# Five token blocks (256, 256, 256, 128, 128 + 32) in place of four (256, 256, 256, 256 + 32) in the front half of a hybrid decoder step

## The reference

```python
h = rms_norm(x, norm1_g)
proj = h @ w_in + b_in
att = windowed_attention(q, k, v, sinks)          # window 128, 8 query heads, 2 kv heads
rw, wkv_t, shift_t = rwkv7_time_mix(proj[...])    # a recurrence over the tokens
merged = gate_a * (att @ w_up_a) + gate_b * (rw @ w_up_b)
x = x + merged @ w_o
h2 = rms_norm(x, norm2_g)
x = x + peer_ffn(h2)      # per token: 8 heads, each picks 16 of 16384 experts by two lists of 128 keys
y = rms_norm(x, final_norm_g)
```

## Time and profile before

| | |
|---|---|
| median of 3 runs | 4102.34 us |
| the profiled execution's own time | 4110.9 us |
| span of its trace | 4109.1 us |
| busy: PE, DVE, POOL, ACT | 79%, 69%, 36%, 35% |
| mean DMA rate over the span | 326 GB/s |
| chain that ended last: PE, DMA, DVE, issue | 23%, 18%, 8%, 6% |

### The profile page before, as it was taken

How to read it: one execution, slowest core, us unless ns; L and a number is a source line. 1 busy time by engine, 2 the same in 40 slices (tenths; PEclk the granted TensorE clock), 3 DMA queues, 4 the chain that set the end, 5 groups by cost and what they waited for, 6 DMA issues and landing times.

```text
span 4109.1 us, 40924 instructions
## 1 busy us (share of the span) xinstructions
PE 3259.7 (79%) x12315; PEld 2054.4 (50%) x12315; DVE 2854.3 (69%) x5892; ACT 1417.6 (35%) x3794; POOL 1478.0 (36%) x1330
## 2 busy tenths in 40 slices
PE   7699779878897788688986975898998867657666
PEld 6487456356655553465654633675554422222221
DVE  1442257878866788798864785795866976688676
ACT  1421123623433346234532353232433332233232
POOL 0210123465323334663331443463322344444443
PEclk9799889989999898899998987997899998998988
DMA  4004699978999899699997995786898999999998
GB/s 152 19 1 134 246 346 372 357 271 318 352 385 406 330 382 360 262 376 376 421 381 303 356 351 204 291 355 257 328 363 322 420 421 421 421 419 417 410 417 331
DMA packets 249647, 1341.30 MB, mean 326 GB/s; under 512 B 32537, under 2 KB 67225, under 8 KB 113474
## 3 DMA queue, kind: packets, MB, share of 16 engines
q0 software_dynamic: 152064, 1107.36, 67.4%
q1 hardware_dynamic: 97362, 231.32, 15.3%
HBM read 1306.90 MB, written 32.70 MB: 326 GB/s over the span
## 4 chain that ended last, share of the span: by engine, by line
PE 23%; DMA 18%; DVE 8%; issue 6%; ACT 2%; POOL 2%; SPq 1%; DVEq 0%; POOLq 0%; ACTq 0%
DMA ring<-in_uv_dram,expert_id 15%; PE acc L2261 8%; PE front L1022 4%; DVE ring L2159 3%; PE front L1077 2%; PE front L766 2%; DVE y_dve L2058 2%; PE front L1040 2%; DMA weights_in<-in_w_all_dram 1%; POOL ring L2033 1%; DMA big<-bonus_gate 0%; ACT diag L2228 0%; PE front L747 0%; DVE ch_xy L1678 0%; DVE ch_alv L1638 0%
## 5 line engine op out<-in xcount | busy, mean ns | idle before, releaser
L2033 POOL DMA_INDIRECT ring<-in_uv_dram,expert_id x1056 | 1224.2, 1159 | 2361.8 <-PE acc L2261 1324.6
L2261 PE MATMUL acc<-ring,diag 128*128 128x512 f32 (+1 forms) x2704 | 1449.3, 678 | 466.8 <-ACT diag L2228 434.7
L2159 DVE CUSTOM_DVE_ANT_0 ring<-ring,h_tile 128x1024 f32<-128x1024 f32 x1056 | 1287.3, 1240 | 264.7 <-DMA ring<-in_uv_dram,expert_id 207.1
L2261 PEld LDWEIGHTS acc<-ring,diag 128*128 128x128 f32 (+1 forms) x2704 | 537.5, 211 | 1183.9 <-ACT diag L2228 577.6
L2058 DVE SCALAR_TENSOR_TENSOR y_dve<-ring,weights,y_dve 128x1024 f32<-128x1024 f32 x371 | 482.7, 1301 | 116.5 <-ACT weights L2216 103.9
L2212 ACT ACTIVATE acts<-dots 128x2 f32<-128x2 f32 x528 | 107.4, 203 | 818.5 <-DVE dots L2159 744.9
L766 PE MATMUL front<-hT,weights_in 128*128 128x257 f32 (+7 forms) x1280 | 304.6, 395 | 18.9 <-DVE hT L1483 18.9
L766 PEld LDWEIGHTS front<-hT,weights_in 128*128 128x128 f32 (+2 forms) x1280 | 243.1, 191 | 88.3 <-DVE hT L1483 21.8
L1077 PE MATMUL front<-h2T,weights_in 128*128 128x256 f32 (+1 forms) x1024 | 250.7, 401 | 31.2 <-DMA weights_in<-in_w_all_dram 30.5
L2216 ACT ACTIVATE weights<-acts,gate 128x1 f32<-128x1 f32 x1056 | 254.1, 288 | 17.4 <-ACT acts L2212 0.2
L2228 ACT ACTIVATE diag<-ident,weights 128x128 f32<-128x128 f32 x651 | 240.2, 390 | 20.5 <-POOLq L521 12.7
(11 more groups left out here) (346 smaller groups left out, 4051.1 us busy)
## 6 DMA issues: line engine op xcount, KB each, us to landing
weights_in<-in_w_all_dram SPq DMA_DIRECT2D x272, 512.0 KB, 7.8
ring<-in_uv_dram,expert_id POOLq DMA_INDIRECT x1056, 11.1
s_unit<-score_rows SPq DMA_DIRECT2D x66, 128.0 KB, 8.2
score_rows<-score_out SPq DMA_DIRECT2D x64, 128.0 KB, 7.8
h_tile<-in_final_g_dram SPq DMA_DIRECT2D x9, 512.0 KB, 8.0
x_rows<-in_x_dram SPq DMA_DIRECT2D x8, 512.0 KB, 12.8
sub_keys<-in_sub_keys_dram SPq DMA_DIRECT2D x4, 1024.0 KB, 19.5
x_rows<-x_rows SPq DMA_DIRECT2D x8, 512.0 KB, 10.1
```

Source lines behind the costliest of these rows:

```text
L2033: e.indirect_dma_start(out=self.ring[:, kk % RING, :], out_offset=None, in_=self.i["uv"], in_offset=bass.IndirectOffsetOnAxis(ap=self.idx[ ...
L2159: n = e.tensor_tensor_reduce(part, part, self.hrow[:, m % 2, :], 1.0, 0.0, ALU.mult, ALU.add, self.dot[:, z, k:k + 1])
L2261: z = e.matmul(self.acc[0:n, d, :], self.diag[:, (at - 1) % 4, 0:n], self.ring[:, kk % RING, D + d * 512:D + (d + 1) * 512], start=first, ...
```

## The change

The block sizes come from a table, and everything that said "2 q", "4 q" or BT now follows it. The front buffers are NX = 256 wide where they were 288; `x_rows` and `score_out` have room for two pieces of tokens in place of three. What that frees in SBUF is used for nothing: unused tensors (`space_0` and the like) grow so that the places that share memory stay where they were, and RING, WBUF and the rest are as before. The core of the diff (where a line of the new code only replaces `2 * q` by `FIRST_TILE[q]` and the like, it is left out):

```diff
-BT = 2 * P
-NBK = TP // BT
-NX = BT + TS
+BLOCK_TILES = (2, 2, 2, 1, 1)
+NBK = len(BLOCK_TILES)
+FIRST_TILE = tuple(sum(BLOCK_TILES[:q]) for q in range(NBK))
+LT = BLOCK_TILES[-1] * P
+NX = max(max(BLOCK_TILES) * P, LT + TS)
...
+def width(q):
+    return prompt(q) + (TS if last(q) else 0)
...
+def lengths(q):
+    n = BLOCK_TILES[q]
+    return dict(zip(NAMES, (10, 66, 32 * n + 6, 30 * last(q), 45, 78 * n + 4, 60 * last(q), 15, 56, 40, 84)))
...
-SHARES = {"qy": (76, 29), "norm": 12, "proj": 105, "att": 120, "datt": 35, "el": 35, "ch": 250, "dec": 110,
-          "out": 15, "merge": 110, "op": 45}
+SHARES = {"qy": ((76, 29), (42, 16)), "norm": (12, 8), "proj": (105, 65), "att": (120, 65), "datt": (35, 35),
+          "el": (35, 24), "ch": (250, 125), "dec": (110, 110), "out": (15, 10), "merge": (110, 60), "op": (45, 30)}
...
+FETCHED = (0, 110, 236, 312, 430)
...
-        end = 104.0 + 122.0 * (q - 1)
...
+        per = (FETCHED[q] - slot) / total
...
+        slot = FETCHED[q]
+        out.append((slot, START[q]["qy"] + HEAD_QY))
...
+def scores_due(u):
+    slot = max(RANKED[u - 2][0] + 1.5, RANKED[u][0] - 2.0)
+    while reached(slot) < scored(u) + 12 and slot < RANKED[u][0] - 0.25:
+        slot += 0.25
+    return slot
...
-            self.xr = s1("x_rows", P, 3, D)
+            self.xr = s1("x_rows", P, 2, D)
...
-            self.sst = s1("score_out", P, 2, 3, 2, NKEY)
+            self.sst = s1("score_out", P, 2, 2, 2, NKEY)
...
-                if tl == 2:
-                    e.wait_ge(self.q_turned, 2 * (m - 2) + 2)
-                    e.wait_ge(self.rows_out[0], 32 * (q + 1))
```

## The result

| | |
|---|---|
| five blocks, median of 4 runs | 4141.61 us (4140.5 to 4153.61) |
| four blocks beside it, median of 4 | 4106.66 us |
| ratio | 1.0087, 95% interval 1.0071 to 1.0103 |
| forecast | 4125 us, 4040 to 4195, slower with 0.53 |
| the profiled execution's own time, and span | 4141.99 us, 4140.2 us |

The change makes the kernel slower by 0.87%, 36 us by the ratio.

A forecast was written before the change was run, and what follows sets the result against it. It took DMA to bound the experts-only tail, and the front beside experts only partly. 2232.0 + 51 + 530 + 885 + 434 = 4132 us of span, 4134 in all, less 8.6: median 4125, range 4040 to 4195.

The forecast's parts named there:

- blocks 1 and 2, 5.9 slots more each: Same work in both blocks plus 5.9 expert slots each at 4.32 us: 51 us later, bounds 27 to 61.
- block 3: New 128-token block with 72.3 slots: stages sum to 525 us, plus 1% for chain and bytes delaying each other, 530.
- block 4: New 160-wide last block with 129.3 slots: stages sum to 869 us, plus 2%, 885.
- tail: Experts alone after the front: 81.5 slots left of 163 at 5.17 us each, 434 us, 421 less than before.
- the larger of two sums: Each block 3 stage takes the larger of its chain (scaled stage plus slots) and its bytes at 400 GB/s.
- 4.32 us for a slot added beside the front: Price of an expert slot beside front work, from blocks 1 and 2: 14.5 slots and 62.7 us between them.
- One more pass of the weights: The fifth block reads 38 MB more: 94 us of DMA at 408 GB/s, nothing if all falls in idle time.
- The two prices behind it: Moving a slot from tail to front returns 0.85 us; against that stand a second set of front latencies and 38 MB.
- Idle time found: Rival: moved slots fill idle DMA time at some 2.7 us each, blocks 3 and 4 under 1380 us, median near 4004; chance 0.27.
- Weight loads come too late: Rival: narrow pieces are used up before four buffers refill in proj, merge, qy; 90 us more, 4215; chance 0.08.
- Narrow matmuls don't shrink: Rival: PE's 128-column matmuls take more than 111 ns in block 3; 50 us more, 4175; chance 0.05.
- The balance: Rival: at 375 to 380 GB/s blocks 3 and 4 take 1387 to 1405 us, gain and cost cancel, 4090 to 4115; chance 0.20.

The follow-up runs named there:

- e2: Changed five-block kernel with block 3's weight loads cut to 8 KB a piece, same instructions and waits: 4103.54 us, ratio 0.9986.
- e12: e1 with block 3's weight loads cut to 8 KB a piece, as in e2: 4203.35 us, ratio 1.0220.
- e7: Four-block kernel before the change with pinned slots 104, 226, 348 replaced by 110, 236, 362, 14 slots moved from tail to front: 4067.72 us, ratio 0.9904.
- e1: Changed five-block kernel with its pin table set so the front ends at the slot where it ended before, 82 slots back in the tail: 4245.22 us, ratio 1.0331.
- e4: Changed five-block kernel with five weight buffers in place of four, same bytes: 4129.56 us, ratio 1.0057.

## Why the prediction was right

It forecast 4125 us, 23 above the kernel before, and gave "slower" a chance of 0.53; measured are 4141.6 and 35 above. The 4125 were a sum of 4134 for one execution, less the 8.6 us by which the profiled execution before lay above its median. The profiled one after took 4142 and lies at its median, so 8 us of the 17 are the sum's and the rest is this step. By its terms, forecast against measured:

| term | forecast | measured |
|---|---|---|
| blocks 1 and 2, 5.9 slots more each | 51 | 34.5 |
| block 3 | 530 | 551.9 |
| block 4 | 885 | 887.4 |
| tail | 434 | 434.4 |

- **The tail** was firm, as it said: slots left and the price of one, both from rows of before.
- **Block 4**, the long term, was 2 us off; dec, for which it took 3.0 us per added slot, came to 154.6 against 153.
- **Block 3** was 22 us short, 2 us outside the 515 to 550 it allowed. Five stages lie within 5 us. Two do not: merge 101.7 against 92, qy 105.9 against 85. The step that was short is "the larger of two sums": qy had bytes alone (34 MB at 400 GB/s) and no chain in that sum. With hardly any weights loaded, e2 still takes 95.8 us there, 23.4 of them behind the column load. Merge's chain, 79 in the sum, is 96.0 there; e12's 69.0 with 7 slots says that the stage alone was scaled well, and that the slots and waits added to it were too cheap. (Proj's chain has a slip: 87.0 less 320 x 0.105 is 53, not 51. Bytes, at 92, set that stage in the sum.)
- **4.32 us for a slot added beside the front** was too dear. It came from blocks 1 and 2, which differ by more than their slots: against the kernel before, the new block 1 takes 35.8 us more for 5.25 slots, and block 2 takes 7.9 us less with 5.5 more. e7 gives 2.4 (5.17 - 2.8) for the first 14. In the changed kernel blocks 1 and 2 have 947 records of dot products where they had 904, 10.75 slots more, and take 27.9 us more, 2.6 each; the other 6.6 us lie in block 0's query projection. The term was too high by 16, which by luck covered three quarters of block 3's 22.
- **One more pass of the weights**, "94 us if nothing idle is found for it, and nothing if it all falls in idle time": 38.4 MB came in, and the weights among them were worth 41 to 46 us (e2, e12).
- In the prediction's last words on the sum, moved slots "give back 421 us" and the front takes "about 444" more: 421.0 and 452.0.
- **The two prices behind it** were both too low, and that they nearly cancel is luck. At 0.85 us a slot 82 slots return 70 us, so the forecast of 23 more puts the fifth block at 93; e1 has 100 and 136, and the difference comes to 36.

The rivals. *Idle time found* was right in its mechanism for the first slots (2.4 us, where it assumed 2.7) and not for the rest. Blocks 3 and 4 took 1439 us together, above its limit of 1380. *Weight loads come too late* had its sign in the profile, 80.4 us of waits in qy where there were 30.5, and e4 showed that taking them away returns 12 us, not 90. *Narrow matmuls don't shrink*: they do, 111 ns at 128 columns. By the Trainium skill ("TensorE: Matmul & The Clock Gate", back-to-back issue gap), with its ratio of 81 to 56, there would have been an estimated 48 us more on PE. In these rows there is no sign of it. *The balance* missed by 26 us.

What stays open is why a slot beside a narrow block costs 4.0 us and more: not the bytes of the weights, since e2 and e12 differ by 4.7 us a slot without them. No run moves slots beside narrow blocks alone at several doses.

## What to carry to other kernels

Price a moved piece of work from both ends, and expect the price to change with where it goes and how much is moved: 14 slots moved beside four wide blocks returned 2.8 us each, and 82 beside five blocks 1.2. Here a further block was paid in bytes for a third only (45 of 136 us), so before adding one to spread work, move the work as far as the present boundaries allow (e7: 39 us for two numbers). A wait that stands out in the profile is an upper bound of what its removal gives: here 77 us of waits for weights gave 12.

## What the hardware showed that was not expected

- A load of 1024 rows of 516 to 1156 bytes took 30 to 41 us to land beside the fetches in the kernel before and the changed one, in no order of size (1156 KB 30.0, 516 KB 40.8), and 8.6 us without them; with fewer slots beside it (e1) it took 12.0 and 22.5. On SyncE's queue it delayed what was issued behind it, an 8 KB load to 23.4 us (e2); from ACT's queue it still took 30 to 33 us itself, and the kernel gained 18 to 27.
- 35.7 MB less to read, at a time when the DMA engines were busy 0.91 of the time, gave back 41 us, half of their 87 at 408 GB/s.
